# A windowed attention whose first key and query products take free PSUM banks in turn, and whose maxima and squares have other places in its schedule

## The reference

```python
# window_attention, 12 heads in 4 groups of 3 that share keys and values
k = rmsnorm(h[..., K part]); q = rmsnorm(h[..., Q part])     # per head, 64 wide
q, k = apply_rope(q), apply_rope(k)                          # latent tokens
for each block i of 128 queries:
    s_ctx = q_i . k_ctx * scale                              # 256 context keys
    s_win = q_i . k[i-1 .. i+1] * scale, masked to |distance| <= 128
    p = softmax([s_ctx, s_win, sink])                        # in float32
    o_i = p_ctx @ v_ctx + p_win @ v
```

## Time and profile before

| | |
|---|---|
| median of 3 runs | 3434.67 us (3431.51 to 3439.59) |
| the profiled execution, its own time | 3439.12 us |
| its span in the trace | 3437.3 us |
| granted TensorE clock, mean over the span | 0.960 |
| `heads1`, start of its first TensorE work to the first attention product | 2235.0 to 2281.9 us |
| `heads1`, the attention itself on TensorE | 2281.9 to about 2580 us |

### The profile page before, as it was taken

How to read it: one execution, slowest core, us unless ns; L and a number is a source line. 1 busy time by engine, 2 the same in 40 slices (tenths; PEclk the granted TensorE clock), 3 DMA queues, 4 the chain that set the end, 5 groups by cost and what they waited for, 6 DMA issues and landing times. The chain is left out here.

```text
span 3437.3 us, 37590 instructions
## 1 busy us (share of the span) xinstructions
PE 3180.9 (93%) x14242; PEld 2180.7 (63%) x14242; DVE 1580.3 (46%) x1955; ACT 1014.9 (30%) x1363; POOL 467.4 (14%) x367
## 2 busy tenths in 40 slices
PE   4987999999897999999999969769998899999998
PEld 1553333333386888888888847624447688888887
DVE  4123544544425445544544471345533555555554
ACT  3013555555413211122111130024543321221221
POOL 0001545555400000000000000024440000000000
PEclk8997999999999999999999989969999999999999
DMA  6920000000201111111111001100001111111111
GB/s 275 378 81 16 4 4 2 3 3 0 81 30 50 38 37 37 37 37 37 37 37 41 19 13 49 40 0 1 1 1 49 65 47 43 43 61 37 49 61 49
DMA packets 34910, 162.27 MB, mean 47 GB/s; under 512 B 3889, under 2 KB 6705, under 8 KB 24754
## 3 DMA queue, kind: packets, MB, share of 16 engines
q1 hardware_dynamic: 34834, 161.24, 13.1%
HBM read 157.03 MB, written 4.19 MB: 47 GB/s over the span
## 5 line engine op out<-in xcount | busy, mean ns | idle before, releaser
L699 PE MATMUL PS<-f_uh,f_Wh 128*128 128x512 f32 (+1 forms) x1760 | 483.1, 372 | 25.8 <-DVE f_ul L436 25.0
L699 PE MATMUL PS<-f_ul,f_Wh 128*128 128x512 f32 (+1 forms) x1760 | 481.6, 371 | 0.0
L699 PE MATMUL PS<-f_uh,f_Wl 128*128 128x512 f32 (+1 forms) x1760 | 481.2, 371 | 0.0
L849 DVE SCALAR_TENSOR_TENSOR X<-PS,mod,X 128x512 f32<-128x512 f32 (+1 forms) x440 | 306.2, 698 | 309.5 <-PE PS L699 309.5
L699 PEld LDWEIGHTS PS<-f_uh,f_Wh 128*128 128x128 f32 x1760 | 307.9, 188 | 89.8 <-issue 19.5
L699 PE MATMUL PS<-f_gh,f_WDh 128*128 128x512 f32 (+1 forms) x880 | 330.9, 376 | 19.5 <-DVE f_gl L835 17.2
L699 PEld LDWEIGHTS PS<-f_ul,f_Wh 128*128 128x128 f32 x1760 | 308.7, 188 | 59.1
L699 PEld LDWEIGHTS PS<-f_uh,f_Wl 128*128 128x128 f32 x1760 | 308.3, 188 | 59.2
L699 PE MATMUL PS<-f_gl,f_WDh 128*128 128x512 f32 (+1 forms) x880 | 326.0, 370 | 0.0
L699 PE MATMUL PS<-f_gh,f_WDl 128*128 128x512 f32 (+1 forms) x880 | 325.3, 370 | 0.0
L818 DVE SCALAR_TENSOR_TENSOR part<-PS,part,part 128x1023 f32<-128x1023 f32 (+1 forms) x132 | 130.0, 1013 | 329.8 <-ACT part L754 329.8
(11 more groups left out here) (255 smaller groups left out, 4300.0 us busy)
## 6 DMA issues: line engine op xcount, KB each, us to landing
part<-in_mod_w SPq DMA_DIRECT2D x48, 1024.0 KB, 7.0
part<-in_w_up SPq DMA_DIRECT2D x88, 512.0 KB, 3.5
part<-in_w_down SPq DMA_DIRECT2D x22, 1024.0 KB, 5.4
part<-in_w_out SPq DMA_DIRECT2D x16, 512.0 KB, 3.5
X<-in_xT SPq DMA_DIRECT2D x4, 1280.0 KB, 9.6
X<-in_xT SPq DMA_DIRECT2D x1, 5120.0 KB, 16.0
part<-in_wqk SPq DMA_DIRECT2D x8, 512.0 KB, 3.6
out<-X SPq DMA_DIRECT2D x16, 256.0 KB, 2.0
```

Of the source, the lines that this page charges most:

```text
L699: mm = pe.matmul(ps(bank + c, hi - lo), w_, x_[:, lo:hi], start=f_, stop=l_)
L849: dve.scalar_tensor_tensor(out=X[:, m, lo:hi], in0=ps(DNB[r % 2], hi - lo), scalar=moda(layer, 5, m, 0 if lo < SEQ else 1), in1=X[:, m, lo ...
```

## The change

Four things are changed, all in `heads1`.

1. Products 1 and 2 of group 0 (`FREE`) write banks 0 and 1, and 2 and 3, instead of 6 and 7. Product q of the first four waits for `out` of product q - 2 only (products 0, 1 and 2 for none).
2. The fifth product of group 0 is moved from UPFRONT to pair 1 (its square to pair 0, its cast to pair 2).
3. The 8 UPFRONT maxima take banks 4, 5 and 2, 3 in turn (`max_bank`), and wait for the maximum two before instead of one before. The matmuls of `rows` now wait for all maxima issued so far.
4. The slots of the later maxima (`STEADY`, `EARLY`) are others: none stands in the side that follows a product's "ro", and the last stands alone in side 0. The squares ("sq") move from side 0 to side 1 of the pair before their product. On GpSimd the casts of a pair stand ahead of its `add` instead of behind it.

```diff
+            FREE = {1: (0, 1), 2: (2, 3)}
...
+            def product(pair, G, w):
+
+                at(pair - 1, 1 if pair > 1 else 0, "sq", G, w)
+                at(pair, 0, "nt", G, w)
+                at(pair, 1, "ro", G, w)
+                at(pair + 1, 0, "ca", G, w)
+
+            def maxima(G, jj, places, row):
+                for t_, (pair, side) in enumerate(places):
+                    at(pair, side, "max", G, jj, t_)
+                at(row, 0, "mn", G, jj)
+                at(row, 1, "row", G, jj)
+            EARLY = [(0, 0), (0, 1), (1, 0), (1, 1), (2, 0), (2, 1), (3, 0), (4, 0)]
+            STEADY = [(0, 0), (0, 1), (1, 0), (2, 0), (2, 1), (3, 0), (3, 1), (4, 0)]
...
                 for w, r in enumerate((-15, -13, -9, -7, -3)):
-                    at(o + r - 1, 0, "sq", G, w)
-                    at(o + r, 0, "nt", G, w)
-                    at(o + r, 1, "ro", G, w)
-                    at(o + r + 1, 0, "ca", G, w)
+                    product(o + r if G else 1 if w == 4 else UPFRONT - 1, G, w)
                 for jj, r in enumerate((-8, -2, 4)):
-                    early = o + r == -2
-                    for t_ in range(8):
-                        if early:
-                            at(t_ // 2, t_ % 2, "max", G, jj, t_)
-                        else:
-                            at(o + r + (0, 1, 2, 2, 3, 3, 4, 4)[t_], (1, 1, 0, 1, 0, 1, 0, 1)[t_], "max", G, jj, t_)
-                    at(4 if early else o + r + 5, 0, "mn", G, jj)
-                    at(4 if early else o + r + 5, 1, "row", G, jj)
+                    if G == 0 and jj < 2:
+                        maxima(G, jj, EARLY if jj else [(UPFRONT, 0)] * 8, 4 if jj else UPFRONT)
+                    else:
+                        maxima(G, jj, [(o + r + d, side) for d, side in STEADY], o + r + 5)
...
+                def banks(G, w):
+                    return FREE.get(NW * G + w, (NB, TB))
+
+                def max_bank(G, jj, qt):
+                    return 2 if (G, jj) == (0, 0) and qt % 2 else RB
...
                         for u in range(NU):
+                            casts(NU * n + u, 0)
                             add(n, u)
-                            casts(NU * n + u, 0)
...
-                        at_least(pe, "out", q)
+                        at_least(pe, "out", q if q > 3 else max(q - 2, 0))
...
-                        at_least(pe, "mc", 24 * G + 8 * jj + qt)
+                        done["max"] += 1
+                        at_least(pe, "mc", done["max"] - (2 if (G, jj) == (0, 0) else 1))
...
                         pe.wait_ge(s["mn"], R + 1)
+                        at_least(pe, "mc", done["max"])
```

More of the change, by code:

```diff
@@ L1794, in _ @@
                         for u in range(NU):
+                            casts(NU * n + u, 0)
                             add(n, u)
-                            casts(NU * n + u, 0)
                 @block.tensor
                 def _(pe):
-                    done = {"nt": 0, "row": 0, "spread": 0}
+                    done = {"nt": 0, "row": 0, "spread": 0, "max": 0}
                     def qk(n, u):
@@ L1857, in norms @@
                         pe.wait_ge(s["sq"], q + 1)
-                        at_least(pe, "out", q)
+                        at_least(pe, "out", q if q > 3 else max(q - 2, 0))
                         at_least(pe, "fin", done["spread"])
-                        pe.matmul(ps(NB, hi - lo), bones, sq[q % 2][:, :hi - lo], start=True, stop=True)
-                        pe.matmul(ps(TB, hi - lo), rot1[:, 1 - t_, :], QK1[:, 2 * G + t_, lo:hi],
+                        nb, tb = banks(G, w)
+                        pe.matmul(ps(nb, hi - lo), bones, sq[q % 2][:, :hi - lo], start=True, stop=True)
+                        pe.matmul(ps(tb, hi - lo), rot1[:, 1 - t_, :], QK1[:, 2 * G + t_, lo:hi],
                                   start=True, stop=True).then_inc(s["nt"], 1)
@@ L1866, in maximum @@
                         pe.wait_ge(s["cast"], NW * G + (3 if jj == 0 else 4 if qt < 4 else 5))
-                        at_least(pe, "mc", 24 * G + 8 * jj + qt)
+                        done["max"] += 1
+                        at_least(pe, "mc", done["max"] - (2 if (G, jj) == (0, 0) else 1))
                         at_least(pe, "mr", done["row"])
+                        rb = max_bank(G, jj, qt)
                         q = qb[JS[jj]][:, qt * P:(qt + 1) * P]
@@ L1872, in maximum @@
                         nk = (hi - lo) * P
-                        pe.matmul(ps(RB, BANK)[:, CTX:BANK], q, k[:, SEQ:T], start=True, stop=True)
-                        pe.matmul(ps(RB + 1, nk), q, k[:, lo * P:hi * P], start=True, stop=False)
+                        pe.matmul(ps(rb, BANK)[:, CTX:BANK], q, k[:, SEQ:T], start=True, stop=True)
+                        pe.matmul(ps(rb + 1, nk), q, k[:, lo * P:hi * P], start=True, stop=False)
                         if qt > 0:
-                            mm = pe.matmul(ps(RB + 1, P), identb[:, :], maskb[:, 0, :], start=False, stop=(qt == 7))
+                            mm = pe.matmul(ps(rb + 1, P), identb[:, :], maskb[:, 0, :], start=False, stop=(qt == 7))
                         if qt < 7:
-                            mm = pe.matmul(ps(RB + 1, nk)[:, nk - P:nk], identb[:, :], maskb[:, 1, :],
+                            mm = pe.matmul(ps(rb + 1, nk)[:, nk - P:nk], identb[:, :], maskb[:, 1, :],
                                            start=False, stop=True)
@@ L1935, in inverse @@
                         at_least(act, "rinv", q)
-                        act.activation(halved(lnb, m), in_halves(ps(NB, m)), ACT.Ln, bias=eps[:, 0:1],
+                        nb, _ = banks(G, w)
+                        act.activation(halved(lnb, m), in_halves(ps(nb, m)), ACT.Ln, bias=eps[:, 0:1],
                                        scale=1.0 / C_HD).then_inc(s["ln"], 1)
                         act.wait_ge(s["ln"], q + 1)
-                        act.activation(in_halves(ps(NB, m)), halved(lnb, m), ACT.Exp, scale=-0.5)\
+                        act.activation(in_halves(ps(nb, m)), halved(lnb, m), ACT.Exp, scale=-0.5)\
                             .then_inc(s["rinv"], 1)
@@ L2034, in rotated @@
                         dve.wait_ge(s["nt"], q + 1)
-                        T_ = ps(TB, m)
+                        nb, tb = banks(G, w)
+                        T_ = ps(tb, m)
                         dve.tensor_tensor(T_, T_, rope[:, 1, lo:hi], ALU.mult).then_inc(s["ts"], 1)
@@ L2046, in rotated @@
                                 op = dve.tensor_tensor(in_halves(dst[0:64, lo:hi]), halved(t1[rows_], m),
-                                                       in_halves(ps(NB, m, rows_)), ALU.mult)
+                                                       in_halves(ps(nb, m, rows_)), ALU.mult)
                         op.then_inc(s["out"], 1)
@@ L2055, in maximum @@
                         lo, hi = WIN[qt]
-                        dve.reduce_max(mc[:, m:m + 1], PS[:, RB * BANK + CTX:(RB + 1) * BANK + (hi - lo) * P], AX_X)\
+                        rb = max_bank(G, jj, qt)
+                        dve.reduce_max(mc[:, m:m + 1], PS[:, rb * BANK + CTX:(rb + 1) * BANK + (hi - lo) * P], AX_X)\
                             .then_inc(s["mc"], 1)
```

## The result

The changed kernel takes 3400.52 us in the median of 4 runs (3397.12 to 3404.19), the kernel before 3435.64 (3431.51 to 3439.59) in as many; the ratio is 0.9898, with a 95% interval from 0.9881 to 0.9915. That is 35.1 us or 1.0% less, against a forecast of 33.6 us and 3401.

What follows compares the result with a forecast made beforehand. TensorE was taken to bound the kernel, busy 93% of the span, with a chain of hand-overs up front. Gains 15.5 + 2.8 + 13.6 + 1.7 = 33.6 us off 3434.7 give 3401.1; range 3391 to 3413.

Steps and rivals of the forecast that it cites:

- The front: Stage start to first attention product: products and maxima up front together gain 15.5 us.
- The maxima: Up front: with two sets of banks the row starts 7.5 us behind the first reduction instead of 14.06, gain 6.6.
- The products: Up front: free banks and the fifth product moved away bring the first reduction from 2265.65 to 2256.7, gain 8.95 us.
- its rise: Up front: rival that the clock comes up there already, 7 us more or 2 if only from the maxima; chance 0.22.
- The ring: Up front: each product waits for its square alone; distances 5.8, 5.6 and 3.65 us at low clock.
- Pairs 0 to 9: Early attention: fifth product costs 1.9 us, new waits 4.0 replace 6.0, a 2.7 clock fall goes; gain 2.8.
- The fall of the clock: Early attention: the slowdown behind the longest waits goes with them, 2.7 us; 0 if the clock falls after all.
- Pairs 10 to 71: Steady attention: TensorE's waits fall from 15.4 to 1.8 us, gain 13.6; the second clock fall goes, gain 1.7.
- product 3 held by its wait for product 1: Up front: a sign named in advance that would show the prediction wrong; no size given.
- the waits come back elsewhere: Attention: rival that half the steady waits and both clock falls stay, giving 3412 us; chance 0.15.
- only the front pays: Whole stage: rival that only the 15.5 us up front is gained, giving 3419 us; chance 0.06.
- GpSimd's order slows the rest: Attention: rival that casts waiting for "ro" make adds and exponentials late, 45 us more, giving 3446; chance 0.03.

Runs made afterwards that it cites:

- products_last: Changed kernel, but TensorE's and ScalarE's product step stands behind the maximum in a shared slot, VectorE's order in side 1 kept: 3397.75 us.
- fifth_up_front: Changed kernel, but the fifth product stands up front again, on banks 6 and 7, waiting for the fourth: 3404.40 us.
- old_maxima_slots: Changed kernel, but the later maxima stand in the slots they had before the change: 3414.84 us.
- front_only: Changed kernel with later maxima, squares and casts put back where they stood before, so only the part up front is changed: 3423.81 us.
- maxima_first: Changed kernel, but where a slot holds a product and a maximum, the maximum stands ahead, VectorE's order turned too: 3407.93 us.
- fifth_in_pair0: Changed kernel, but maxima stand ahead of products in shared slots and the fifth product is in pair 0 instead of pair 1: 3402.27 us.
- later_only: Changed kernel with the front put back as before, so only later slots, squares and the order of casts and adds are changed: 3411.47 us.
- casts_behind_adds: Changed kernel, but GpSimd's casts of a pair stand behind its add again: 3398.45 us.

## Why the prediction was right

The sum came out 1.1 us short of the stage's 34.7, from 2.0 too little up front and 0.9 too much behind it, which partly cancel. That the median lies within 0.6 us of the forecast of 3401.1 is luck to that extent, the more so as the four single times stand between 3397 and 3404.

**The front, 15.5 predicted, 17.5 measured.** The maxima: 6.6 predicted, and from the first reduction to the row 7.35 after 14.06, so 6.7. The products: 8.95 predicted. The first reduction came 30.65 behind the first product before (2265.65 less 2235.00) and 19.90 after (2250.79 less 2230.89): 10.75. This term was sized 1.8 too small. The step that erred is the one that kept the clock at its low level up front: I gave its rise 0.22 as a rival, with 2 to 7 us. It took place in part, in all eleven profiled executions with the free banks, each time for a few us only. The rival had it come up for good, behind the first product (7 us) or from the maxima on (2 us), so that its lower figure is met in size and not in mechanism. The ring that I described (each product waiting for its square, 5.8 us apart, then 5.6 and 3.65) was measured as 5.3, 4.7 and 3.6; the clock was up in the end of the first product and the start of the second, and again in the end of the fourth. Where the first rise came later, in `products_last`, the distances were 5.7, 5.5 and 2.7: the first is the ring as reckoned, and the third is short because the clock was up in the half-width product.

**Pairs 0 to 9, 2.8 predicted, 2.1 measured.** The waits were predicted as 2.0 in pair 2 and 0.85 and 1.15 in pair 4, and read as 1.8, 0.9 and 1.2, with one more of 0.4 (the second in the line "1.2, 2, 0.9"). Product 4 costs what was said: `fifth_up_front` has 4.0 us less here, against 1.9 + 2.0. The fall of the clock was gone, as said; since the same wait of 1.8 was followed by a fall in `old_maxima_slots`, and in none of six other runs that have it, this was likely and not sure.

**Pairs 10 to 71, 15.3 predicted, 15.1 measured.** Waits of 0.5 in three places were left (0.45 predicted; the two others of 0.1 don't show), and the second fall of the clock did not come. Following VectorE's list slot by slot, with the durations of before, was enough for this. What I had not seen is which of the three edits did it: the slots are enough alone, with the squares' and the casts' places worth 0.3 and nothing once these are as they are.

**Two descriptions ahead of the prediction are wrong.** The later maxima do stand in the side that follows a product's "ro" (pairs 10, 12 and 16, side 0, for instance). What the new slots avoid, but for pair 1, is side 1 of the product's own pair, in which the "ro" itself stands. The prediction's reckoning of the steady part goes by the slots as they are and does not suffer. And product 3 waits until `out` is 1, which product 0 raises, and not for product 1; so the sign "product 3 held by its wait for product 1" could not have come.

**The falls of the clock.** I took them away with the long waits, with 4.4 us at stake. The Trainium skill, TensorE: Matmul & The Clock Gate, "A second HAM failure mode: psum-queue depth-cycling", spoke for their staying. In the attention the trace does not bear it out: at 0.5 us of waits now and then the clock is 1.00 for 234 us. Up front, where pauses of 1.5 to 2 us stand between products and the banks do go round, it swings between its levels in the windows above, much as the Trainium skill tells; yet that was a gain, since before it never came up at all. Over the runs, the falls in the attention beyond its first few us all stand in or just behind a wait of 1.75 us or more (before, `front_only`, `old_maxima_slots`, `maxima_first`, `fifth_in_pair0`), and in `old_maxima_slots` fourteen waits of 0.6 to 1.4 in 242 us brought none. The converse does not hold: of three waits of 2.14 before only one was followed by a fall, and the 1.8 in the changed kernel by none. What decides between them was not tried.

**The rivals.** That the waits come back elsewhere, that only the front pays, and that GpSimd's order slows the rest are excluded by `later_only`, `front_only` and `casts_behind_adds`.

## What to carry to other kernels

When TensorE waits ahead of small matmuls whose result another engine must take off, write down that other engine's list slot by slot and keep its long steps out of the place in front of the reduction that TensorE needs next; here the slots of the maxima were worth 15.5 us of 35, with no work removed. Up front, where nothing else runs beside the chain, a second set of banks for the maxima took 6.75 us off it; the banks came from what stood idle in that phase. Whether one would pay inside the attention was not tried. When a slot's order is changed, change it for one engine at a time: the same exchange won 2 us of the stage on TensorE alone, and lost 4 when VectorE made it too, a fall of the clock included.

## What the runs showed that I had not expected

The same `turn` (128 x 512, two inputs in SBUF) took anything from 0.75 to 2.76 us, and the length follows from what GpSimd was doing when it began. Over the fourteen traces there are 224 such turns. Where no cast or addition of GpSimd had more than about 0.2 us still to run, the turn took 0.75, also when an addition began 0.12 us or more behind its start, and also beside a memset. In the others the turn ended 0.54 to 0.56 us after the GpSimd instruction did (in six of them, after the addition that followed at once):

| GpSimd's instruction runs on for, us | 0.25 | 0.42 | 0.63 | 0.68 | 0.95 | 2.21 |
|---|---|---|---|---|---|---|
| the turn takes, us | 0.80 | 0.97 | 1.18 | 1.23 | 1.50 | 2.76 |

The 2.21 is the addition in `maxima_first` above, which had started 0.14 before the turn. In the changed kernel two additions end at 2290.15, and the turn beside them at 2290.70:

```profile
2288.08 2.07 POOL L1800 TENSOR_TENSOR part<-part,part 128x384 f32<-128x384 f32 x2
...
2289.89 0.81 DVE L2043 SCALAR_TENSOR_TENSOR X<-part,sml,part 128x512 f32<-128x512 f32 x1
```

So the turn stood still until the GpSimd instruction was over. The Trainium skill, SBUF — State Buffer, "SBUF: two separate sides", says that VectorE with two SBUF inputs and a GpSimd instruction that reads SBUF take a shared pair of ports by an exclusive lock, the later one blocking until the first instruction ends; the trace agrees with all of these figures. It means that the price of a VectorE step in such a schedule depends on which GpSimd addition it happens to meet, and can be reckoned from where it meets it.

Up front, the clock came up for short stretches between the products in all eleven runs with the free banks, and in none of the three without. The first two pauses of TensorE between the products are 1.7 to 2.0 us with the banks and 3.0 without. So closing a pause by 1 us in each of two rings, reckoned at 2.1 us, came with 3.3 to 3.9 to the first maximum.
